# The first gather without the gate's wait, and an expert's combination moved later in its successor

## The reference

```python
def moe_ffn(h, router_w, router_b, w1, w3, w2):
    logits = h.astype(jnp.float32) @ router_w.astype(jnp.float32) + router_b.astype(jnp.float32)
    top_v, top_i = lax.top_k(logits, TOP_K)
    top_w = jax.nn.softmax(top_v, axis=-1)
    combine = jnp.sum(jax.nn.one_hot(top_i, N_EXPERTS, dtype=jnp.float32) * top_w[..., None], axis=-2)
    ...
    for e in range(N_EXPERTS):
        y = y + combine[..., e:e + 1] * swiglu(h, w1[e], w3[e], w2[e])
```

## Time and profile before

| | us |
|---|---|
| median of 3 executions | 1628.99 (1627.79 to 1629.59) |
| the profiled execution | 1628.33 |
| its span, first to last instruction | 1626.5 |
| TensorE busy in the span | 1551.4 (95%) |
| VectorE busy | 1312.0 (81%) |
| ScalarE busy | 973.8 (60%) |
| experts, from the first matmul of unit 0 (606.96) to the end of the last combination (1615.39) | 1008.4 |

### The profile page before, as it was taken

How to read it: one execution, slowest core, us unless ns; L and a number is a source line. 1 busy time by engine, 2 the same in 40 slices (tenths; PEclk the granted TensorE clock), 3 DMA queues, 4 the chain that set the end, 5 groups by cost and what they waited for, 6 DMA issues and landing times.

```text
span 1626.5 us, 19533 instructions
## 1 busy us (share of the span) xinstructions
PE 1551.4 (95%) x7955; PEld 1278.4 (79%) x7955; DVE 1312.0 (81%) x1187; ACT 973.8 (60%) x854; POOL 44.0 (3%) x116
## 2 busy tenths in 40 slices
PE   5999799999899969999999999999999999999996
PEld 5885689999788548887887887887887887887885
DVE  5887787888664358799899889989989989979986
ACT  1432334444344327777686687777777777777775
POOL 5200100000000000000000000000000000000000
PEclk9998899999999979999999999999999999999998
DMA  9854678887814138999999999999999989999990
GB/s 356 292 199 164 232 286 323 311 308 273 291 59 156 52 130 324 338 368 347 330 364 354 360 335 347 361 339 346 361 340 346 366 329 360 360 336 359 347 355 28
DMA packets 157142, 481.05 MB, mean 296 GB/s; under 512 B 4218, under 2 KB 6438, under 8 KB 157046
## 3 DMA queue, kind: packets, MB, share of 16 engines
q1 hardware_dynamic: 155120, 475.02, 79.3%
q0 software_dynamic: 1392, 3.58, 0.6%
q10 hardware_dynamic: 534, 1.13, 0.2%
HBM read 478.66 MB, written 1.05 MB: 295 GB/s over the span
## 4 chain that ended last, share of the span: by engine, by line
PE 85%; DVE 9%; ACT 2%; issue 2%; DMA 2%; SPq 0%; DVEq 0%; ACTq 0%
PE bank L1086 18%; PE bank L1088 17%; PE bank L1087 17%; PE bank L798 4%; PE bank L1012 3%; PE bank L1014 3%; PE bank L1013 3%; PE bank L983 3%; PE bank L795 3%; DVE ring_low L1676 2%; PE bank L1060 2%; DMA ring<-in_w_mod_dram 2%; PE bank L1027 2%; PE bank L1028 2%; PE bank L1029 2%
## 5 line engine op out<-in xcount | busy, mean ns | idle before, releaser
L1676 DVE TENSOR_TENSOR ring_low<-ring,w_high 128x2048 fp32r<-128x2048 f32 x336 | 766.7, 2292 | 116.1 <-ACT w_high L2058 108.0
L2058 ACT ACTIVATE w_high<-ring 128x2048 fp32r<-128x2048 f32 x336 | 646.3, 1924 | 245.8 <-PE bank L1088 238.0
L1086 PE MATMUL bank<-w_high,x_high 128*128 128x512 f32 x896 | 355.8, 397 | 5.2 <-DVE ring_low L1676 3.9
L1087 PE MATMUL bank<-ring_low,x_high 128*128 128x512 f32 x896 | 355.3, 397 | 0.0
L1088 PE MATMUL bank<-w_high,x_low 128*128 128x512 f32 x896 | 353.1, 394 | 0.0
L1086 PEld LDWEIGHTS bank<-w_high,x_high 128*128 128x128 f32 x896 | 168.7, 188 | 48.5 <-DVE ring_low L1676 7.3
L1088 PEld LDWEIGHTS bank<-w_high,x_low 128*128 128x128 f32 x896 | 168.2, 188 | 37.9
L1087 PEld LDWEIGHTS bank<-ring_low,x_high 128*128 128x128 f32 x896 | 168.4, 188 | 36.3
L2000 ACT ACTIVATE tmp_r<-ring 128x1024 fp32r<-128x1024 f32 x84 | 89.1, 1063 | 149.1 <-PE bank L1014 89.4
L1088 PE MATMUL bank<-w_high,act_low 128*128 128x512 f32 x448 | 178.0, 397 | 0.0
L1086 PE MATMUL bank<-w_high,act_high 128*128 128x512 f32 x448 | 177.1, 395 | 0.3 <-DVE ring_low L1676 0.3
(11 more groups left out here) (323 smaller groups left out, 1691.4 us busy)
## 6 DMA issues: line engine op xcount, KB each, us to landing
ring<-in_moe_w_dram SPq DMA_DIRECT2D x168, 2048.0 KB, 7.9
ring<-in_w_mod_dram SPq DMA_DIRECT2D x23, 2048.0 KB, 10.8
ring<-in_ffn_w_dram SPq DMA_DIRECT2D x21, 2048.0 KB, 13.7
ring<-in_w_in_dram SPq DMA_DIRECT2D x8, 2048.0 KB, 17.6
ring<-in_w_out_dram SPq DMA_DIRECT2D x4, 2048.0 KB, 8.4
ring<-in_w_mod_dram SPq DMA_DIRECT2D x2, 1024.0 KB, 16.0
gate_row<-in_b_mod_dram POOLq DMA_DIRECT2D x4, 512.0 KB, 7.3
ring<-in_w_in_dram SPq DMA_DIRECT2D x2, 1024.0 KB, 11.3
```

What stands on the lines that cost most here:

```text
L1086: mm(out_, x_h, w_h, start=first, stop=False)
L1087: mm(out_, x_h, w_l, start=False, stop=False)
L1676: tt_(moe_low(u, m // 2)[:, c], moe_slot(u, m // 2)[:, c], w_high[:, m % HIGHS, :].bitcast(F32), ALU.subtract).then_inc(low_made, 1)
L2058: act(w_high[:, m % HIGHS, :], moe_slot(u, m // 2)[:, c], ACT.Copy).then_inc(high_made, 1)
```

## The change

In words:

- **First gather.** The wait for the gate leaves `routing()` and stands in `experts(0)` behind both gathers, ahead of unit 0.
- **VectorE's pieces of the combination.** The two gate products stood together ahead of `low(2)`, the two `y_low` behind it. Now it is: `low(2)`, gate product of half 0, `low(3)`, `y_low` 0, `low(4)`, gate product of half 1, `low(5)`, `y_low` 1. The sums, two behind unit 6 and two behind unit 7 before, stand one behind unit 10, two behind 11, one behind 12. The products of the first two groups (L1715) move from units 10 and 11 to 9 and 10, the next expert's mask (`dispatch_of`) from 12 to 13.
- **ScalarE's pieces.** `y_high` of half 0 behind `high(3)`, of half 1 behind `high(5)` (both stood behind `high(2)`). The copy of the mask moves from unit 10 to unit 13.
- **TensorE.** The combination moves from between units 3 and 4 to between 7 and 8, the mask's transposes from before unit 8 to between 9 and 10, and there they wait for the sum of c00 (its bank is now 7, and that of c01 is 6).
- **End.** Behind the last expert VectorE does gate product and `y_low` of half 0, then those of half 1.
- **Count of the second pass.** VectorE and ScalarE read `most_i` ahead of the experts, SyncE between the transfers of the second and third expert; the branch stays where it was. TensorE's is unchanged.

Its hunks in order: the table of banks and the step names; SyncE; TensorE's routing and experts; TensorE's expert; VectorE's expert; the end of VectorE's experts; the count, on VectorE and ScalarE; ScalarE's expert. `up(..., middle)` calls `middle()` ahead of its second half.

```diff
-COMBINE = ((0, 0, 6), (1, 0, 4), (0, 1, 7), (1, 1, 5))
+COMBINE = ((0, 0, 7), (1, 0, 4), (0, 1, 6), (1, 1, 5))
...
-        ("yg0 yg1 yl0 yl1").split(),
+        ("yg0 yl0 yg1 yl1").split(),
...
+                    if q == 0 and c == 2 * NCH:
+                        eng.wait_ge(route_v.sem, route_v.at("most_i"))
+                        most_tokens.append(eng.value_load(most_i[0:1, 0:1], min_val=0, max_val=T))
...
-                eng.wait_ge(gate_v.sem, gate_v.at("g1", 2 * DEPTH - 1))
...
                 if q == 0:
+                    eng.wait_ge(gate_v.sem, gate_v.at("g1", 2 * DEPTH - 1))
                     for g in range(NE // PAIR):
...
+                def spread_turn():
+
+                    if not is_first(q, g, u):
+                        eng.wait_ge(sum_v.sem, sum_v.at("a00", old))
+                    for tt in range(TT):
+                        ins = nc.tensor.transpose(bank[7][:, tt * P:(tt + 1) * P], dispatch[:, u, tt, :], ident)
+                    mark(ins.then_inc(moe_t.sem, 1), moe_t, "spread")
+
                 up(0, "w1", 0)
                 if is_first(q, g, u):
                     eng.wait_ge(route_v.sem, route_v.at("most"))
-                else:
+                up(0, "w3", 2)
+                if not is_first(q, g, u):
                     combine(old)
-                up(0, "w3", 2)
-
+
+                eng.wait_ge(moe_a.sem, moe_a.at("s1", r))
+                up(1, "w1", 0, spread_turn)
                 if not is_first(q, g, u):
                     eng.wait_ge(sum_v.sem, sum_v.at("a01", old))
-                for tt in range(TT):
-                    ins = nc.tensor.transpose(bank[7][:, tt * P:(tt + 1) * P], dispatch[:, u, tt, :], ident)
-                mark(ins.then_inc(moe_t.sem, 1), moe_t, "spread")
-
-                eng.wait_ge(moe_a.sem, moe_a.at("s1", r))
-                up(1, "w1", 0)
                 turn(0)
                 eng.wait_ge(moe_a.sem, moe_a.at("spread", r))
                 turn(1)
...
                     for m in range(UNITS):
-                        if m == 2 and not first:
-                            y_gates(old, q, r)
                         if not first or m >= HIGHS:
                             low(r, u, m)
-                        if m == 2 and not first:
-                            y_lows(old)
-                        if m == 6 and not first:
-                            sums(old, old_weight, slice(0, 2))
-                        if m == 7 and not first:
-                            sums(old, old_weight, slice(2, 4))
-                        if m in (10, 11):
-                            product(m - 10)
-                        if m == 12:
+                        if m in (2, 4) and not first:
+                            y_gate((m - 2) // 2, old, q, r)
+                        if m in (3, 5) and not first:
+                            y_rest((m - 3) // 2, old)
+                        if m == 10 and not first:
+                            sums(old, old_weight, 0)
+                        if m == 11 and not first:
+                            sums(old, old_weight, 1, 2)
+                        if m == 12 and not first:
+                            sums(old, old_weight, 3)
+                        if m in (9, 10):
+                            product(m - 9)
+                        if m == 13:
                             if q:
...
-                y_gates(end, q, expert(q, 0, NE))
-                y_lows(end)
-                sums(end, choice[:, 1, 2, :] if q else chosen[:, 2, NE - 1, :], slice(0, 4))
+                for half in range(2):
+                    y_gate(half, end, q, expert(q, 0, NE))
+                    y_rest(half, end)
+                sums(end, choice[:, 1, 2, :] if q else chosen[:, 2, NE - 1, :], 0, 1, 2, 3)
...
+            with_more = eng.value_load(most_i[0:1, 0:1], min_val=0, max_val=T) > SLOTS
...
-                        if m == 2 and not first:
-                            y_highs(old)
+                        if m in (3, 5) and not first:
+                            y_first((m - 3) // 2, old)
                         if m in (6, 7):
                             gated(m - 6)
-                        if m == 10:
+                        if m == 13:
                             eng.wait_ge(moe_t.sem, moe_t.at("spread", r))
```

More of the change, by code:

```diff
@@ L557, in _ @@
                     eng.dma_start(dst, src).then_inc(landed[n % RING], 16)
+            most_tokens = []
             def load_pass(q):
@@ L589, in _ @@
             load_pass(0)
+            with_more = most_tokens[0] > SLOTS
             store(0)
-            eng.wait_ge(route_v.sem, route_v.at("most_i"))
-            with eng.If(eng.value_load(most_i[0:1, 0:1], min_val=0, max_val=T) > SLOTS):
+            with eng.If(with_more):
                 load_pass(1)
@@ L1088, in three, with up @@
                     return mm(out_, x_l, w_h, start=False, stop=last)
-                def up(J, name, first):
+                def up(J, name, first, middle=None):
                     n_j = len(GROUPS_OF[J])
@@ L1095, in up @@
                     for half in range(n_j):
+                        if half and middle:
+                            middle()
                         if J == 0 and name == "w1":
@@ L1677, in low, with y_gate, y_rest, sums @@
                     ALU.subtract).then_inc(low_made, 1)
[L1679 to L1698, removed]
+            def y_gate(half, rep, q, r):
+                if half == 0 and isinstance(r, int) and r == NE and q == 0:
+                    eng.wait_ge(half_t.sem, half_t.at("y"))
+                else:
+                    eng.wait_ge(unit_used, used_at(r, -1))
+                done(eng, tt_(act_m[:, half, :], bank[4 + half][:, :], gate_row[:, half * W:(half + 1) * W],
+                              ALU.mult).then_inc(comb_v.sem, 1), comb_v, f"yg{half}", rep)
+            def y_rest(half, rep):
+                c = slice(half * W, (half + 1) * W)
+                eng.wait_ge(comb_a.sem, comb_a.at(f"yh{half}", rep))
+                done(eng, tt_(y_low[:, c], act_m[:, half, :], y_high[:, c].bitcast(F32),
+                              ALU.subtract).then_inc(comb_v.sem, 1), comb_v, f"yl{half}", rep)
+            def sums(rep, weight, *which):
+                for tt, half, b in (COMBINE[n] for n in which):
                     eng.wait_ge(comb_t.sem, comb_t.at(f"c{tt}{half}", rep))
@@ L2058, in high, with y_first @@
                 act(w_high[:, m % HIGHS, :], moe_slot(u, m // 2)[:, c], ACT.Copy).then_inc(high_made, 1)
[L2060 to L2064, removed]
+            def y_first(half, rep):
+                eng.wait_ge(comb_v.sem, comb_v.at(f"yg{half}", rep))
+                done(eng, act(y_high[:, half * W:(half + 1) * W], act_m[:, half, :], ACT.Copy).then_inc(comb_a.sem, 1),
+                     comb_a, f"yh{half}", rep)
             def two_experts(q, g):
@@ L2138, in experts @@
                         two_experts(q, g)
-                y_highs(combined(q, expert(q, 0, NE)))
+                for half in range(2):
+                    y_first(half, combined(q, expert(q, 0, NE)))
             def final(rep):
```

2 lines of the change are left out of this document (1 added, 1 removed).

## The result

The changed kernel takes 1618.87 us (median of 4 executions, 1617.32 to 1619.59), the kernel before 1629.29 in the same comparison (1627.79 to 1632.33): ratio 0.9932, 95% interval 0.9915 to 0.995. The medians differ by 10.4 us, the ratio says 11.1; forecast were 8.4 less than before. The way and most of the size came true, but the gain is larger than the sum, and by the ratio (0.9932 x 1628.99 = 1617.9) the time lies 0.4 us under the lower end of the range. The measured median itself, 1618.87, lies 0.6 us inside it: the two ways of stating the result differ by more than the distance to the edge.

A forecast was written before the change was run, and what follows sets the result against it. TensorE was taken to set the pace over the experts (busy 986 of 990 us). Terms 3.4 + 5.0 + 0 = 8.4 us off the profiled 1628.33 gave 1619.9; predicted median 1620.3, range 1618.3 to 1625.

The forecast's parts named there:

- Part 1: Ahead of the experts: without the gate's wait the first gather starts 3.4 us earlier; bounds 1.5 and 3.6.
- Both register loads: Early loads of `most_i` on ScalarE and VectorE around the first gather: hidden, by 0.9 and 1.9 us.
- Part 2: In the experts: TensorE's 0.82 us stall at unit 3 goes, seven times, 0.1 allowed back: 5.0 us; bounds 2 and 5.7.
- the rival of a late VectorE: VectorE late at unit 15 or 6, 0.3 to 0.7 us seven times: 1622.5 to 1625.5 us; chance 0.2.
- the mask's copy: ScalarE's copy behind `high(13)`: cost 0; as a rival, one unit late, 19 us slower, 1639; chance of slower 0.03.
- Part 3: After the last expert: new order of halves and register loads leaving the end bring 0 us.
- the new order of the halves: VectorE's work behind the last expert: first sum again at 1614.27, gain 0, hidden by the second half's own chain.

The follow-up runs named there:

- e7: Changed kernel with VectorE's and ScalarE's pieces of the combination together around unit 2 as before: 1625.78 us, ratio 0.9985 to the kernel before.
- e6: Changed kernel with VectorE's making of the next expert's mask behind unit 16 in place of 13: 1615.91 us, ratio 0.9929 to the kernel before.
- e9: Changed kernel without the second pass and without its branch on every engine: 1618.46 us, one execution.
- e3: Kernel before with VectorE's register load alone moved ahead of the experts: 1625.26 us, one execution.
- e5: Changed kernel with VectorE's register load alone put back to the end: 1620.59 us, ratio 0.9944 to the kernel before.
- e4: Kernel before with VectorE's register load at its end done twice: 1630.35 us, one execution.
- e2: Changed kernel with the gate's wait and all three register loads where they stood before: 1623.96 us, ratio 0.9959 to the kernel before.
- e1: Kernel before with only the gate's wait moved behind the first gather: 1623.62 us, ratio 0.9962 to the kernel before.

## Why the prediction fell short

**Part 1, first gather: right, 3.4 forecast, 3.5 measured.** The chain behind it moved whole; the clock came back with it, 4.6 to 4.7 us behind the gather's start in both kernels. With the rule of the Trainium skill that was weighed there (page "TensorE: Matmul & The Clock Gate", section "Part 1: The HAM clock gate": half rate is the default, activity releases it), the trace agrees. Both register loads were hidden; they took 0.54 us (VectorE) and 0.46 us (ScalarE), less than the 0.83 assumed.

**Part 2, experts: right in its mechanism, 5.0 forecast, 5.4 in the changed kernel (999.20 against 1004.56).** Per expert 0.9 us go up to unit 11 (0.82 expected; 1.2 in the second expert) and 0.2 come back at unit 15 (0.1 expected), so that 5.0 came near 5.4 with both of its parts somewhat too small. By experts the second gives 1.0, the next five 0.6 to 0.7 each, the last 0.9. e7 shows that the order of VectorE's and ScalarE's pieces was the cause at unit 3, e6 that the mask's place is the cause at unit 15. The last expert, which makes no mask, has no such wait in the changed kernel either. So the rival of a late VectorE came true at its place, with less than its smallest price of 0.3 us; the mask's copy was never late.

**Part 3, the end: this step failed.** The prediction said: "The registers' loads leave the end. They lay beside the last stores' flight, so 0". That is true of SyncE's, and not of VectorE's. The load's row stood among the rows, at 1622.0 with 0.83 us, but I took the last stores for the last thing that the end waits for, and never asked when each engine reaches the closing barrier. VectorE reached it last. Its instructions on the line of the branch, in the kernel before, beside the load in the earlier trace rows:

```profile
L1858 DVEq FUSED_REGOPS  x1: 222/222/222, 1622.8 to 1622.8; - x1
...
L1858 DVEq COMPARE_BRANCH  x1: 72/72/72, 1623.2 to 1623.2; - x1
```

The jump is done at 1623.2 and the next instruction, the drain, starts at 1626.2: 3.0 us with nothing in between; without the jump past the second pass (e9) the drain is 0.23 behind the last product. The Trainium skill, page "Runtime: NRT & Kernel Launch", section "🔬 Instruction fetch mechanics", says that a taken jump out of the prefetched window stalls the engine until the target is fetched; the trace agrees in kind, and the 3.0 us are this trace's. With the load's 1.1 us ahead of it, VectorE came at 4.26 us behind its last product and SyncE at 2.96. The load is worth its 1.1 us only until SyncE is last, and in the changed kernel SyncE, with its stores, came at 3.24: hence 1.0. e3, e5 and e4 turn it off and on in both kernels: 14.0, 14.9, 15.7. The other half of Part 3, that the new order of the halves brings nothing, was right (e2 against e1).

**The sum.** 3.5 + 5.4 + 1.0 = 9.9, against 3.4 + 5.0 + 0: of the 1.5 us that the sum was short, the end is 1.0 and the experts 0.4. The differences of medians for this kernel were 10.4, 9.9 and 9.5 us in three comparisons, and the ratios 0.9932, 0.9929 and 0.994, which are 11.1, 11.6 and 9.8 us. So by its stretches the change does 9.9. What is above it in two of the ratios is inside their intervals. In e1's it is not: 6.2 us, with an interval from 4.1, where its stretches give 3.6, and at least 0.5 us of that stay unexplained. The stretch ahead of the masks, which no edit touches, went from 594.39 to 599.90 in thirteen profiles, and a few executions may not average that out; that this is the reason is not shown.

The range went 2.0 us below the forecast and 4.7 above it, where the rivals lay. A term set to 0 because something else was believed to be last needed its own size as the lower bound, 1 us; with the 3.6 and 5.7 of the other bounds the lower end would have been 1628.3 - 10.3 = 1618.0, which the ratio's 1617.9 still passes by a hair. By the stretches alone the time would be 1629.0 - 9.9 = 1619.1, inside the range. So on which side of its edge the result fell was settled by scatter; the missing microsecond at the end was not.

What stays open: why TensorE's starts are 0.233 us apart behind the stall and 0.231 without it, which makes most of the 0.08 us per expert beyond the 0.82 and of the 0.15 in e7; the 0.3 us more in the second expert; the 0.5 us in e1; and why the stores landed sooner in e9.

## What to carry to other kernels

In all thirteen profiles the span ended 0.2 to 0.3 us after the last engine reached the closing barrier, whichever engine that was. Before calling anything at the end free because stores are in flight, look at the drain of every engine, with the jump that it takes on the way. On an engine that feeds the bounding one with little to spare, it is the sum of the pieces between two of its deliveries that counts, not its busy share (81% here): put one piece between two deliveries, and walk on to the next place without a pause, since the lateness saved at unit 3 was partly paid at unit 15. And a wait that guards something used later (the gate's banks, first written by unit 0) belongs at that use.

## What the runs showed of the hardware

- Behind its taken jump past the second pass, VectorE's next instruction started 3.0 us later (1623.2 to 1626.2, before), and 2.8 to 3.3 us later in all twelve profiles with that jump. In the seven profiles in which no load stands in between, its drain came 3.1 to 3.4 us behind its last product; without that jump, 0.23. ScalarE's next instruction came 2.65 us behind its jump (1620.2 to 1622.9, before); SyncE's after 1.3 us at most (1623.5 to 1624.7), where it also had the stores to wait for.
- The last stores of 256 KB landed 2.7 to 3.0 us after their issue in twelve profiles (median of two each), and 2.3 us after it in e9, which has no jumps past the second pass.
- A load of one number from SBUF into a register took 0.83 to 0.85 us on VectorE just behind its products, 0.54 between them (early, in the changed kernel), and 0.58 as the second of two; on ScalarE 0.46 to 0.47; on SyncE 0.47 between transfers and 0.70 to 0.72 at the end.
- A `low` of 128x2048 float32 is shown with 2.29 us of its own, and the next instruction on VectorE starts 2.21 behind it (730.72 to 732.93 in the changed kernel).
